# A hybrid decoder layer: S5 taps stored by group, its outputs in two banks, GELU rows back by quarters

## The reference

```python
bu = jnp.einsum('gph,blgh->blgp', b_bar, uf.astype(jnp.complex64))
a_cum, h = lax.associative_scan(lin_combine, (a_seq, bu), axis=1)
h = h + a_cum * h0[:, None]
y = jnp.real(jnp.einsum('ghp,blgp->blgh', c_mat, h)) + d * uf
g = jax.nn.gelu(y.reshape(bsz, l, B_WIDTH))
gv = g @ w_glu
return gv[..., :B_WIDTH] * jax.nn.sigmoid(gv[..., B_WIDTH:]), h[:, -1]
...
y_prompt = rmsnorm(xp, final_norm_w)
```

## Time and profile before

| | us |
|---|---|
| median of 3 runs | 1910.81 |
| lowest and highest | 1900.81, 1911.44 |
| the profiled execution | 1898.15 |
| its span | 1896.5 |
| TensorE busy | 1821.8 (96%) |
| VectorE busy | 687.3 (36%) |
| ScalarE busy | 377.7 (20%) |
| GpSimd busy | 505.1 (27%) |

### The profile page before, as it was taken

How to read it: one execution, slowest core, us unless ns; L and a number is a source line. 1 busy time by engine, 2 the same in 40 slices (tenths; PEclk the granted TensorE clock), 3 DMA queues, 4 the chain that set the end, 5 groups by cost and what they waited for, 6 DMA issues and landing times.

```text
span 1896.5 us, 28609 instructions
## 1 busy us (share of the span) xinstructions
PE 1821.8 (96%) x11549; PEld 1751.6 (92%) x11549; DVE 687.3 (36%) x1402; ACT 377.7 (20%) x913; POOL 505.1 (27%) x483
## 2 busy tenths in 40 slices
PE   6999999999999999899899999999999999999996
PEld 6899899999988888788799999999999999999996
DVE  6836711405423444676764251121111111111125
ACT  5211112242113221443402141100110011001111
POOL 5762112222221111111122232233222322332231
PEclk9999999999999998899999999999999999999998
DMA  5563243232232222433354312233223322342233
GB/s 185 91 134 113 80 140 113 94 89 90 90 115 79 91 79 100 131 119 119 112 193 147 105 62 88 93 118 111 89 88 102 120 89 100 100 134 99 88 118 129
DMA packets 80832, 205.69 MB, mean 108 GB/s; under 512 B 15360, under 2 KB 35072, under 8 KB 80488
## 3 DMA queue, kind: packets, MB, share of 16 engines
q1 hardware_dynamic: 38240, 90.52, 15.1%
q0 software_dynamic: 20912, 72.39, 12.0%
q10 hardware_dynamic: 21592, 41.56, 6.7%
HBM read 179.05 MB, written 24.48 MB: 107 GB/s over the span
## 4 chain that ended last, share of the span: by engine, by line
PE 83%; DVE 6%; issue 4%; POOL 3%; ACT 2%; DMA 2%; ACTq 0%; SPq 0%; DVEq 0%; POOLq 0%
PE ps L1076 25%; PE ps L1077 24%; PE ps L1078 24%; POOL SP L853 1%; POOL WL L828 1%; PE ps L1274 1%; PE ps L1414 1%; PE ps L1277 1%; DVE HL L2055 1%; PE ps L1445 1%; PE ps L1450 1%; DVE X L2063 1%; DMA WH<-in_w 1%; POOL WL L1014 1%; PE ps L1497 1%
## 5 line engine op out<-in xcount | busy, mean ns | idle before, releaser
L1076 PE MATMUL ps<-HL,WH 128*128 128x384 f32 (+1 forms) x2496 | 826.8, 331 | 15.3 <-DVE HL L2055 6.5
L1077 PE MATMUL ps<-HH,WL 128*128 128x384 f32 (+1 forms) x2496 | 812.8, 326 | 0.0
L1078 PE MATMUL ps<-HH,WH 128*128 128x384 f32 (+1 forms) x2496 | 811.0, 325 | 0.0
L1076 PEld LDWEIGHTS ps<-HL,WH 128*128 128x128 f32 x2496 | 474.5, 190 | 28.1 <-issue 15.0
L1077 PEld LDWEIGHTS ps<-HH,WL 128*128 128x128 f32 x2496 | 474.9, 190 | 0.2
L1078 PEld LDWEIGHTS ps<-HH,WH 128*128 128x128 f32 x2496 | 474.3, 190 | 0.0
L828 POOL TENSOR_TENSOR WL<-WRAW,WH 128x1024 fp32r<-128x1024 f32 x136 | 328.1, 2413 | 481.5 <-DMA WH<-in_w 478.5
L825 POOL DMA_DIRECT2D WH<-in_w x136 | 78.8, 579 | 808.4 <-PE ps L1078 796.6
L2055 DVE TENSOR_TENSOR FM<-FS,ps 128x384 f32<-128x384 f32 (+1 forms) x66 | 34.3, 521 | 436.8 <-PE ps L1078 432.8
L1076 PE MATMUL ps<-FL,WH 128*128 128x384 f32 (+1 forms) x528 | 171.4, 325 | 6.6 <-POOL WL L828 6.6
L1078 PE MATMUL ps<-FH,WH 128*128 128x384 f32 (+1 forms) x528 | 170.9, 324 | 0.0
(11 more groups left out here) (316 smaller groups left out, 1674.6 us busy)
## 6 DMA issues: line engine op xcount, KB each, us to landing
WRAW<-in_w SPq DMA_DIRECT2D x145, 512.0 KB, 3.2
WH<-in_w POOLq DMA_DIRECT2D x136, 512.0 KB, 3.6
gate_scratch<-GT ACTq DMA_DIRECT2D x24, 528.0 KB, 3.0
PX<-gate_scratch ACTq DMA_DIRECT2D x24, 528.0 KB, 3.6
X<-in_x ACTq DMA_DIRECT2D x8, 528.0 KB, 4.2
X<-in_x SPq DMA_DIRECT2D x16, 192.0 KB, 4.7
u_scratch<-UF ACTq DMA_DIRECT2D x4, 528.0 KB, 4.4
GF<-gelu_scratch SPq DMA_DIRECT2D x4, 528.0 KB, 5.7
```

The source lines that it names most:

```text
L1076: nc.tensor.matmul(out, wh, rl, start=start, stop=False)
L1077: nc.tensor.matmul(out, wl, rh, start=False, stop=False)
L1078: return nc.tensor.matmul(out, wh, rh, start=False, stop=stop)
```

## The change

KTS becomes [P, group, time step, 16], so that the weights of a group lie side by side. The unshifted taps go to a part of CDG (`TAPS[0]`), which is free by then. One DMA instead of seven makes a copy shifted by 16 rows (`TAPS[1]`), and twelve ScalarE copies (`taps_in_steps`) place the taps from one or the other into KTS, between the evictions of gates 3 and 4.

`outputs(b, half)` takes two pairs at a time. In each it runs both KTS products and then the OFF products of the two row halves in turn. Row half 0 writes bank 5 and row half 1 bank 6, with no fence between them. GELU has eight calls of two activations. All S5 work of TensorE moves back by a chunk or more among the gates, so that the first taps come after chunk 1 of gate 0 instead of chunk 0, and the last outputs after chunk 0 of gate 10 instead of gate 9.

`gelu_stores` works in quarters (48 DMAs instead of 24, half as large). Three of the four GF rows are loaded after the third quarter, and the GLU waits for each row by itself. On GpSimd the squarings move: unit 6 is split ahead of part 0, and the loads of units 7 and 8 are issued one part ahead of their splits. SyncE loads raw unit 7 ahead of the taps' shift. In the last norm chunk 2 takes banks 4 and 3, and VectorE's scaling is spread around chunk 2's steps. `padGF` moves GF, GGH and GGL in memory.

```diff
-    KTS = sb(p1, "KTS", [P, SUB, 16, NG])
+    KTS = sb(p1, "KTS", [P, NG, SUB, 16])
...
+    TAPS = [CDG[:, i, :, :, :].rearrange("p a e h -> p (a e) h") for i in range(2)]
...
-    def chunk_sums_at(n):
-        return bank[7 - n % 2][:, 496 + 4 * n:500 + 4 * n]
-    def chunk_spread_at(n):
-        return bank[6 + n % 2]
+    def chunk_sums_at(n, q=2):
+        return (bank[4] if q == 3 and n == 2 else bank[7 - n % 2])[:, 496 + 4 * n:500 + 4 * n]
+    def chunk_spread_at(n, q=2):
+        return bank[3] if q == 3 and n == 2 else bank[6 + n % 2]
...
+        if n == 2 and q == 2:
+            nc.tensor.wait_ge(cn_used, 1)
...
+        first_weights(7)
         sp.wait_ge(tap_ev, 1)
-        for t in range(SUB - 1):
-            sp.dma_start(KTS[0:(t + 1) * 16, t, :, :], KTS[(SUB - 1 - t) * 16:P, SUB - 1, :, :]).then_inc(s_kt, 16)
-        first_weights(7)
+        sp.dma_start(TAPS[1][0:P - 16], TAPS[0][16:P]).then_inc(s_kt, 16)
...
-        def gelu_stores(half):
-            sp.wait_ge(gelu_ok, 8 * (half + 1))
-            g0, ng = half * NG // 2, NG // 2
+        def gelu_stores(b):
+            sp.wait_ge(gelu_ok, 2 * (b + 1))
+            g0, ng = b * NG // 4, NG // 4
...
+        def gelu_load(j):
+            sp.dma_start(GF[:, j, :], gscr[j * P:(j + 1) * P, :]).then_inc(s_gf, 16)
+        for u in range(8, 13):
             first_weights(u)
         gelu_stores(0)
+        first_weights(13)
+        first_weights(14)
+        gelu_stores(1)
         first_weights(15)
+        gelu_stores(2)
+        sp.wait_ge(st_mm, 4)
+        sp.wait_ge(sb_mm, 1)
+        sp.wait_ge(s_gyst, 36 * 16)
+        for j in range(3):
+            gelu_load(j)
         first_weights(16)
-        gelu_stores(1)
-        sp.wait_ge(s_gyst, 24 * 16)
-        for j in range(4):
-            sp.dma_start(GF[:, j, :], gscr[j * P:(j + 1) * P, :]).then_inc(s_gf, 16)
+        gelu_stores(3)
         first_weights(17)
+        sp.wait_ge(s_gf, 48)
+        sp.wait_ge(s_gyst, 48 * 16)
+        gelu_load(3)
...
+        def split_begun(u):
+            pool.wait_ge(acc_done[2], TILE_END[u - 2])
+            nc.gpsimd.dma_start(WH[:, u % 2, :], io["w"][u]).then_inc(s_high[u % 2], 16)
+        def split_ended(u):
+            pool.wait_ge(s_raw[u % 2], 16 * (u // 2 + 1))
+            pool.wait_ge(s_high[u % 2], 16 * (u // 2 - 2))
+            nc.gpsimd.tensor_tensor(WL[:, u % 2, :], WRAW[:, u % 2, :], WH[:, u % 2, :].bitcast(F32),
+                                    ALU.subtract).then_inc(split_ok, 1)
...
+            if u == FIRST:
+                split_begun(6)
+                split_ended(6)
                 s5_squarings(0)
-            if u == 7:
+                split_begun(7)
                 s5_squarings(1)
-            if u == 8:
+                split_ended(7)
                 s5_squarings(2)
+                split_begun(8)
                 s5_squarings(3)
+                split_ended(8)
...
-        def output(b, j):
-            if j == 0:
+        def outputs(b, half):
+            p = 2 * b + half
+            if half == 0:
                 pe.wait_ge(hst_ok, b + 1)
-                if b == 0:
-                    pe.wait_ge(s_kt, 7 * 16)
-                    pe.wait_ge(off_ok, 1)
-            pr = 4 * b + j
-            if pr >= 2:
-                pe.wait_ge(gelu_ok, pr - 1)
-            for e in range(2):
-                g = 2 * pr + e
-                o = bank[5 + pr % 2][:, 256 * e:256 * e + YC]
-                nc.tensor.matmul(o, KTS[:, :, :, g].rearrange("p t h -> p (t h)"), U[:, g, 0:YC], start=True, stop=False)
-                if e == 1:
-                    fence_wait()
-                nc.tensor.matmul(o, OFF_re[64 * e:64 * e + 64, pr, :], HST[64 * e:64 * e + 64, 0, j, :],
-                                 start=False, stop=False)
-                last = nc.tensor.matmul(o, OFF_im[64 * e:64 * e + 64, pr, :], HST[64 * e:64 * e + 64, 1, j, :],
-                                        start=False, stop=True)
-                if e == 0:
-                    fence_set(last)
+            if p == 0:
+                pe.wait_ge(kt_ok, 1)
+                pe.wait_ge(off_ok, 1)
+            else:
+                pe.wait_ge(gelu_ok, p)
+            for i in range(2):
+                j = 2 * half + i
+                pr = 4 * b + j
+                o = [bank[5 + e][:, 256 * i:256 * i + YC] for e in range(2)]
+                for e in range(2):
+                    g = 2 * pr + e
+                    nc.tensor.matmul(o[e], KTS[:, g, :, :].rearrange("p t h -> p (t h)"), U[:, g, 0:YC], start=True, stop=False)
+                for part, off in ((0, OFF_re), (1, OFF_im)):
+                    for e in range(2):
+                        r = 64 * e
+                        last = nc.tensor.matmul(o[e], off[r:r + 64, pr, :], HST[r:r + 64, part, j, :],
+                                                start=False, stop=part == 1)
             last.then_inc(y_mm, 1)
...
+        gate(0, [0, 1])
+        taps(0)
+        gate(0, [2])
+        taps(1)
+        gate(1, [0])
+        taps(2)
+        gate(1, [1])
+        taps(3)
+        gate(1, [2])
+        stt_rows(0)
         for n in range(3):
-            gate(0, [n])
-            taps(n)
-        gate(1, [0])
-        taps(3)
-        gate(1, [1])
-        stt_rows(0)
-        gate(1, [2])
-        stt_rows(1)
-        gate(2, [0])
-        stt_rows(2)
-        gate(2, [1])
-        stt_rows(3)
-        gate(2, [2])
+            gate(2, [n])
+            stt_rows(n + 1)
+        gate(3, [0])
         step_sums(0, 0)
-        gate(3, [0])
+        gate(3, [1])
         step_sums(0, 1)
-        gate(3, [1])
+        gate(3, [2])
...
-        gate(4, [2])
+        for n in range(3):
+            gate(4, [n])
+            sample_sums(n + 1)
+        gate(5, [0])
         step_sums(1, 0)
-        gate(5, [0])
+        gate(5, [1])
         step_sums(1, 1)
-        gate(5, [1])
-        output(0, 0)
+        outputs(0, 0)
         gate(5, [2])
-        output(0, 1)
-        for b in range(3):
-            gate(6 + b, [0])
-            output(b, 2)
-            output(b, 3)
-            gate(6 + b, [1])
-            if b < 2:
-                step_sums(b + 2, 0)
-            output(b + 1, 0)
-            gate(6 + b, [2])
-            if b < 2:
-                step_sums(b + 2, 1)
-            output(b + 1, 1)
-        gate(9, [0])
-        output(3, 2)
-        output(3, 3)
-        gate(9, [1, 2])
-        gate(10)
+        outputs(0, 1)
+        gate(6, [0, 1])
+        step_sums(2, 0)
+        gate(6, [2])
+        step_sums(2, 1)
+        outputs(1, 0)
+        gate(7, [0])
+        outputs(1, 1)
+        gate(7, [1, 2])
+        step_sums(3, 0)
+        gate(8, [0])
+        step_sums(3, 1)
+        outputs(2, 0)
+        gate(8, [1])
+        outputs(2, 1)
+        gate(8, [2])
+        gate(9)
+        outputs(3, 0)
+        gate(10, [0])
+        outputs(3, 1)
+        gate(10, [1, 2])
...
+            before = (lambda n, k: pe.wait_ge(gg_lo, k + 1)) if i == 0 else None
+            unit(u, u % 2, [((no, 0, 4, GGH, GGL), dict(before=before)), ((no + 1, 4, 4, GGH, GGL), {})])
...
+        def taps_in_steps(ts):
+            for t in ts:
+                late = SUB - 1 - t
+                if late % 2:
+                    act.wait_ge(s_kt, 16)
+                else:
+                    act.wait_ge(tap_ev, 1)
+                r0, rows = 16 * (late - late % 2), 16 * (t + 1)
+                step = 32 if r0 == 32 else rows
+                for r in range(0, rows, step):
+                    n = min(step, rows - r)
+                    last = nc.scalar.copy(KTS[r:r + n, :, t, :], TAPS[late % 2][r0 + r:r0 + r + n])
+            if ts[-1] == 0:
+                last.then_inc(kt_ok, 1)
+        def gelu(p):
+            act.wait_ge(y_mm, p + 1)
+            y = ps_all[:, 5:7, :].rearrange("p e (i c) -> p i e c", i=2)[:, :, :, 0:YC]
+            u = U[:, 4 * p:4 * p + 4, 0:YC].rearrange("p (i e) c -> p i e c", e=2)
+            for i in range(2):
+                last = nc.scalar.activation(u[:, i], y[:, i], ACT.Gelu_apprx_tanh)
+            last.then_inc(gelu_ok, 1)
+        def gelu_high(js, loaded):
+            act.wait_ge(s_gf, 16 * loaded)
+            for j in js:
+                nc.scalar.copy(as_blocks(GGH[:, j, :], NBLK), as_steps(GF[:, j, :], 0, NBLK))
+                nc.scalar.copy(GGH[:, j, SEQ:T], GF[:, j, SEQ:T]).then_inc(gg_hi, 1)
...
+        gate(3, [0])
+        taps_in_steps([7, 5])
+        gate(3, [1])
+        taps_in_steps([3, 1, 6])
+        gate(3, [2])
+        taps_in_steps([4])
+        gate(4, [0])
+        taps_in_steps([2, 0])
+        gate(4, [1, 2])
...
+        gate(10, [1])
+        gelu_high([0, 1, 2], 3)
         gate(10, [2])
         gate(11, [0])
-        act.wait_ge(s_gf, 64)
-        for j in range(4):
-            nc.scalar.copy(as_blocks(GGH[:, j, :], NBLK), as_steps(GF[:, j, :], 0, NBLK))
```

(12 more changed lines are left out.)

## The result

The changed kernel takes 1874.93 us (median of 4, 1871.1 to 1875.21), the kernel before beside it 1906.36 (median of 4): ratio 0.9835, 95% interval 0.9811 to 0.986. That is faster by 1.65%; 1875 was forecast. Run again later it took 1871.38 (median of 6), ratio 0.9823 (0.9792 to 0.9853).

A forecast was written before the change was run, and what follows sets the result against it. TensorE, busy 96% of the span, was taken as the bound. 16.6 + 7.7 + 0.9 + 4.0 + 1.7 + 1.7 = 32.6 us off the runs' mean of 1907.7 gave 1875, range 1868 to 1882, with rivals 1861 to 1890.

The forecast's parts named there:

- outputs: TensorE's output products: faster KTS loads, fewer height changes and alternating row halves save 16.6 us, bounds 6 and 20.
- first taps: TensorE's wait for W at the first taps goes, 4.3 us, and the low clock behind it, 3.4; together 7.7.
- ScalarE's queue, gate 0's store: Sample loads of U issued before gate 0's last eviction: cost nothing, or 4 to 5 us if the queue freed no sooner.
- split weights: Two TensorE waits (2.2 us) and a low clock spell (1.7) go, 3 us left for waits or clock: gain 0.9 us.
- GLU: Wait for split GELU rows ahead of the GLU and low clock behind it: 4.0 of 4.7 us saved.
- clock in the bursts: Low clock spells after bursts of output pairs, 3.4 us: half taken, 1.7 us saved, bounds 0 and 3.4.
- last norm: VectorE's 1.73 us idle for the root of chunk 2 is filled with scalings: 1.7 us saved.
- loads' layout: In the outputs, KTS weight loads without the 32-element stride save about 0.10 us each, 6.4 us in all.
- changes of height: In the outputs, the array empties between full and half height; two changes a pair instead of two a group save 6.4 us.
- alternation: In the outputs, OFF products alternating between row halves bring loads closer together: 3.8 us saved, bounds nothing and 7.
- rival that had 0.06: In the outputs, weight loads of the two row halves run wholly side by side: 3 us more, 1872 us; chance 0.06.
- splits or ScalarE's queue late: GpSimd's split chain slips 8 us, gain 26, 1882 us, or ScalarE's queue frees late, 4 to 5 us; chance 0.15.

The follow-up runs named there:

- strided run: The changed kernel with KTS laid out as before, a group's operand read with a stride of 32 elements; 1882.5 us, run once.
- half-by-half run: The changed kernel with each pair's OFF products re, im of the upper 64 rows, then of the lower, instead of in turn; 1868.46 us, run once.
- two lots on time: The changed kernel with SyncE's U loads in lots of three and five, the second after unit 6's split, sample loads after gate 1's first third; 1866.14 us.
- store first: The changed kernel with gate 0's last third evicted and its store issued on ScalarE ahead of the sample loads of U; 1867.62 us.
- late sample loads: The changed kernel with ScalarE's sample loads of U behind gate 1 and the first transposes' eviction, unit 8's split ahead of the third squarings; 1870.81 us.

## Why the prediction held, point by point

| step | predicted | by the two profiles |
|---|---|---|
| outputs | 16.6 | 20.3 |
| first taps | 7.7 | 7.5 |
| ScalarE's queue, gate 0's store | 0 | -9.4 |
| split weights | 0.9 | 3.9 |
| GLU | 4.0 | 4.7 |
| clock in the bursts | 1.7 | 2.7 |
| last norm | 1.7 | 2.1 |
| sum | 32.6 | 31.8 |

The medians differ by 31.4. The two spans differ by less, 23.5: the profiled execution of before was 8 us under its median, and the changed one came 3.8 us later to the first gate (75.55 instead of 71.76), in a part that the change doesn't touch. The part behind the stretch, from the first GLU matmul to the end, was even 1.1 us longer (1598.7 instead of 1597.6), though the table has 3.5 us saved there (1.4 of the GLU's 4.7, and the norm's 2.1). In the changed kernel and its versions, except for the one with GELU in halves, this part took 1595 to 1602 us, so these 4.6 us are within what it varies by, and no run shows the 3.5 in the total.

So the total was right partly by luck: 9.4 us of loss that the sum had at nothing were made up by the outputs (3.7 more than forecast), the split weights (3.0) and three smaller terms (2.1), less 0.2 at the taps.

- *Outputs.* The loads' layout was sized right (6.4; 6.6 by the strided run), and so were the changes of height (6.4; 0.43 x 16 = 6.9). The failed term is the alternation: 3.8, when the halves run wholly side by side and it is the upper bound, 0.44 x 16 = 7. The 0.08 us between loads of the scores was the wrong row to go by: the scores' eight matmuls of 256 columns took 1.14 us, longer than the 0.73 of their loads, so the loads' spacing there is not their own; the rival that had 0.06 was what happened. The Trainium skill (TensorEngine Tiling (Array Packing), Key Properties) states both halves of this, the emptying at a change of mode and the parallel loads, and the runs agree with both: 0.2 us for a change of height, and a second half's four loads at no time of their own. And the reason given, "alternate between the row halves", is wrong: the half-by-half run shows that the order doesn't matter.
- *First taps.* From gate 0's first matmul to the end of chunk 1 and the first taps it took 89.76 - 71.76 = 18.0 us before and 86.09 - 75.55 = 10.5 after. But "without a pause it has no cause" held only until gate 2: the 7.2 us wait there brought the low clock back, and with the taps moved back the stretch grew by 1 to 3 us only. Before the change gate 3 began 127.89 - 71.76 = 56.1 us after gate 0, with 1.1 us of step sums ahead of it, and after it 55.5: in these first gates the store's wait took back all that the taps and the weights had gained.
- *ScalarE and SyncE.* "I cost this at nothing; if the queue freed no sooner than before, it is 4 to 5 us." This is the step that failed. The bound named the right place and was too small, because it counted ScalarE's issues alone. The eviction's 16.9 us of waiting for the landing, and the like delay of unit 6's weights, come from SyncE's U loads, whoever issues behind them: with three of the eight ahead instead of all, the store landed in 5.5 us and the weights in 7.0. "The load has a queue of its own" was no protection. The prediction called itself wrong from a wait of 8 us for evicted banks on; it was 7.2, and 9.4 with the clock. So the rival "splits or ScalarE's queue late" (0.15) came true here, and its 1882 did not only because other terms gave more. The earlier trace rows had the sign: a DMA share of 1.24 at 106 GB/s.
- *Split weights.* The 3 us left for a late chain didn't come, since the store's wait covered it; the gain is the 1.4 us wait at gate 2 (113.23) and 2.5 at gate 4 with the clock behind it. In the runs where that cover was gone, 0.9 to 2.8 us showed at gate 3, and where the loads of U stood ahead of the weights 2.4 at gate 2.
- *GLU, norm.* The 3.3 us of waits went, and so did the low spell of 1.4 behind them; 274.28 to 284 us ran at 1.00. The tail from 1872.27 to 1893.07 us took 20.8, now 18.75. The first GLU matmul came at 274.28 instead of 268: 3.8 of it the late start. In the bursts no low spell is left (190 to 200 at 1.00). Their 2.7 is a remainder: with gates 0 to 4 and all sample sums done it was 298.86 - 162.20 = 136.66 us to the GLU, now 274.28 - 163.91 = 110.37, and 26.3 - 20.3 - 3.3 = 2.7.

## What to carry to other kernels

A DMA that something waits for can land 17 us after its issue, instead of 7, although it is alone in its queue. When the DMA share is over 1 at a low rate (here 1.24 at 106 GB/s), look for the loads in small packets, and put the urgent transfers ahead of them or cut them into lots. Put products over half the rows next to each other, without a full-height product between them; their own order is free. When a stall at one place is removed, price the next thing that is late in its shadow before the gain is booked.

## What the runs showed of the hardware

- TensorE's two row halves took their products independently, even ahead of the program's order: eight loads of 64x128 in the time of four, in banks of their own.
- A load of 128x128 fp32 weights 32 elements apart took 303 ns, a contiguous one 189, and they followed each other at 0.21 and 0.11 us.
- One issue of a 16 KB load on ScalarE took 0.3 to 0.5 us, one of them 1.8, with three of U's large loads landed before (two lots on time). With all eight under way the first few took as little, and later ones up to 7.4 us (store first) and 8.3 (before the change).
- Nearly all in packets of 512 B, U's loads moved 105 GB/s from 87 to 96 us (late sample loads), with the sixteen engines busy all the time.
- The clock behind a wait isn't told by the wait's length. After 7.2 us without work its mean was 0.62, more at 1.2 than at 2.4 GHz, after 2.4 us (late sample loads) 0.71, and after 3.0 us (store first) 1.00, all at 2.4. After 2.8 us at gate 3, in the run with late sample loads too, it was 1.00:

```profile
106.50:112.30 5.80, 5.73 (x24) 5.74 (x25) 0.00 (x0) 0.00 (x0) 4.76 (x25) 0.71 0.78 141
125.44:129.85 4.41, 4.41 (x25) 4.16 (x25) 2.52 (x19) 0.00 (x0) 3.72 (x18) 1.00 0.72 237
```

```profile
106.80:112.00 5.20, 5.14 (x33) 5.14 (x33) 0.00 (x0) 2.16 (x6) 4.33 (x22) 1.00 0.62 188
```
